# Adaptive modulation as a row product with an accumulating VectorE step, in a fused two-block transformer kernel

## The reference

```python
c_act = jax.nn.silu(c)                       # (1, 1024)
mod = jnp.einsum('bd,de->be', c_act, w_ada[l]) + b_ada[l]      # w_ada (1024, 6144)
shift_m, scale_m, gate_m, shift_f, scale_f, gate_f = jnp.split(mod, N_MOD, axis=-1)
h = (_rms(x) * (1.0 + scale_m) + shift_m)
...
x = x + gate_m * jnp.einsum('bse,ed->bsd', mixed, w_out[l])
h = (_rms(x) * (1.0 + scale_f) + shift_f)
u = jnp.square(jax.nn.relu(jnp.einsum('bsd,df->bsf', h, w_mlp_in[l])))
x = x + gate_f * jnp.einsum('bsf,fd->bsd', u, w_mlp_out[l])
```

## Time and profile before

| | |
|---|---|
| median of 3 runs | 836.43 us (834.17 to 836.99) |
| profiled execution, its own time | 834.69 us |
| its span, first to last instruction | 832.9 us |
| PE busy | 798.2 us, 6530 matmul records |
| PEld busy | 782.2 us |
| DVE busy | 625.4 us, 977 instructions |
| ACT busy | 377.0 us |
| DMA | 155.6 MB, mean 187 GB/s |
| mean granted clock of PE | 0.982 of full |

### The profile page before, as it was taken

How to read it: one execution, slowest core, us unless ns; L and a number is a source line. 1 busy time by engine, 2 the same in 40 slices (tenths; PEclk the granted TensorE clock), 3 DMA queues, 4 the chain that set the end, 5 groups by cost and what they waited for, 6 DMA issues and landing times.

```text
span 832.9 us, 15451 instructions
## 1 busy us (share of the span) xinstructions
PE 798.2 (96%) x6530; PEld 782.2 (94%) x6530; DVE 625.4 (75%) x977; ACT 377.0 (45%) x504; POOL 27.7 (3%) x27
## 2 busy tenths in 40 slices
PE   8997998998899999999999999999989899999998
PEld 8997997898898999999999999989889899999998
DVE  5957586876975778999997888967767778855563
ACT  6656334553755633343335553445446533434331
POOL 0000000002101000000000000300010000000000
PEclk9999997999999999999999999999899999999999
DMA  9854442221734447787886425554215257745521
GB/s 338 297 192 149 146 161 102 102 103 52 295 110 153 153 155 304 282 308 270 294 305 240 174 102 191 210 206 153 102 52 203 102 207 300 282 173 202 174 80 52
DMA packets 23972, 155.60 MB, mean 187 GB/s; under 512 B 3552, under 2 KB 3680, under 8 KB 5856
## 3 DMA queue, kind: packets, MB, share of 16 engines
q1 hardware_dynamic: 23904, 154.61, 51.3%
HBM read 153.55 MB, written 1.05 MB: 186 GB/s over the span
## 4 chain that ended last, share of the span: by engine, by line
PE 73%; DVE 11%; issue 8%; ACT 6%; DMA 1%; POOL 1%; SPq 0%; DVEq 0%; POOLq 0%; ACTq 0%
PE bank L740 13%; PE bank L742 13%; PE bank L741 13%; PE bank L809 7%; PE bank L812 7%; PE bank L811 7%; DVE sb_lo L1664 3%; ACT sb_hi L1339 3%; PE bank L748 2%; PE bank L1202 2%; PE bank L750 1%; PE bank L751 1%; DMA sb_raw<-in_stream 1%; PE bank L1226 1%; PE bank L1169 1%
## 5 line engine op out<-in xcount | busy, mean ns | idle before, releaser
L1664 DVE TENSOR_TENSOR sb_lo<-sb_raw,sb_hi 128x2048 fp32r<-128x2048 f32 (+1 forms) x116 | 261.6, 2258 | 96.8 <-ACT sb_hi L1339 96.4
L1339 ACT CAST sb_hi<-sb_raw 128x2048 fp32r<-128x2048 f32 (+1 forms) x116 | 217.5, 1880 | 112.1 <-PE bank L812 55.6
L740 PE MATMUL bank<-sb_u_hi,sb_hi 128*128 128x256 f32 (+2 forms) x800 | 230.9, 289 | 2.8 <-issue 2.8
L742 PE MATMUL bank<-sb_u_hi,sb_lo 128*128 128x256 f32 (+2 forms) x800 | 228.1, 285 | 0.0
L741 PE MATMUL bank<-sb_u_lo,sb_hi 128*128 128x256 f32 (+2 forms) x800 | 227.3, 284 | 0.0
L740 PEld LDWEIGHTS bank<-sb_u_hi,sb_hi 128*128 128x128 f32 (+2 forms) x800 | 152.4, 191 | 6.3 <-issue 5.5
L742 PEld LDWEIGHTS bank<-sb_u_hi,sb_lo 128*128 128x128 f32 (+2 forms) x800 | 152.9, 191 | 0.2
L741 PEld LDWEIGHTS bank<-sb_u_lo,sb_hi 128*128 128x128 f32 (+2 forms) x800 | 152.9, 191 | 0.3
L809 PE MATMUL bank<-sb_hid_hi,sb_hi 128*128 128x256 f32 x432 | 121.3, 281 | 0.4 <-DVE sb_hid_lo L1718 0.4
L812 PE MATMUL bank<-sb_hid_hi,sb_lo 128*128 128x256 f32 x432 | 120.8, 280 | 0.0
L811 PE MATMUL bank<-sb_hid_lo,sb_hi 128*128 128x256 f32 x432 | 120.5, 279 | 0.0
(11 more groups left out here) (352 smaller groups left out, 1229.5 us busy)
## 6 DMA issues: line engine op xcount, KB each, us to landing
sb_raw<-in_stream SPq DMA_DIRECT2D x140, 1024.0 KB, 5.0
sb_raw<-in_stream SPq DMA_DIRECT2D x4, 256.0 KB, 6.5
sb_raw<-in_stream SPq DMA_DIRECT2D x2, 512.0 KB, 9.2
sb_mem_t<-in_mem SPq DMA_DIRECT2D x1, 1024.0 KB, 4.9
out<-sb_h SPq DMA_DIRECT2D x4, 256.0 KB, 2.1
sb_const<-in_constants SPq DMA_DIRECT2D x1, 830.0 KB, 10.4
sb_h<-in_x SPq DMA_DIRECT2D x1, 576.0 KB, 3.8
sb_h<-in_x SPq DMA_DIRECT2D x1, 512.0 KB, 6.9
```

The costliest lines, as they stand in the source:

```text
L740: nc.tensor.matmul(out, a_hi, b_hi, start=(i == 0), stop=False)
L742: last = nc.tensor.matmul(out, a_lo, b_hi, start=False, stop=(i == n - 1))
L1339: nc.scalar.copy(hi[:, s % SPLIT, 0:n], x[:, 0:n]).then_inc(sem("hi_ready"), 1)
L1664: tt(lo[:, s % SPLIT, 0:n], x[:, 0:n], f32(hi[:, s % SPLIT, 0:n]), ALU.subtract) \
```

## The change

w_ada is laid out the other way round on the host: a block still holds 256 outputs, but the output is on the partition and the 1024 input features lie along it, two groups of 128 outputs beside each other. The row c is loaded into all 128 partitions (`c_row`, 128 by 1024, one DMA) and ACT applies silu to it. `ada(j)` on DVE is now two instructions, each 128 by 1024: the block times `c_row`, written back over the block, with the sum along the row written to one column of `mod`. The matmuls with ones and the DVE step behind them go; the biases are added by three instructions (`ada_bias`). The two pieces of the first projection go into the feed-forward, one more in round 2 and one more in round 9, so that rounds 2 to 9 have two each. `tail_t` and `logit_t` become views of a part of `summed`, to make room.

```diff
-    ada, summed = iter(range(24)), []
+    ada = iter(range(24))
     def more_ada():
-        if len(summed) == 2:
-            add("ada_sum", summed.pop(0))
         for j in ada:
             raw.append(("ada", j))
             add("ada", j)
-            summed.append(j)
             return
...
-    add("c_act")
     block("proj", 0, evac_now=False, ahead=False)
...
-    more_ada()
     block("proj", 3)
     add("rstd_row", 0)
     add("turn_qk", 0)
-    more_ada()
     block("proj", 4)
...
         if i == 1:
             add("hidden", hidden.pop(0))
+            add("c_act")
+            add("weigh_cols")
         if 2 <= i <= 9:
             more_ada()
         block("ffn_in", 2 * i + 1)
-        if 3 <= i <= 8:
+        if 2 <= i <= 9:
             more_ada()
         block("ffn_out", i - 1, hidden_first=i == 10)
         if i == 8:
+            add("ada_bias", 0, 12)
             add("mod", 0)
...
     block("proj2", 14, between=[("pv", 16), ("pv", 17)])
-    while summed:
-        add("ada_sum", summed.pop(0))
     steps([("turn_p", 18), ("turn_p", 19), ("scores", 20), ("scores", 21), ("mix_scale", 0, 1), ("mix_tanh", 0),
-           ("mod", 1), ("shift", 1)])
+           ("ada_bias", 12, 20), ("mod", 1), ("shift", 1)])
...
-        if 7 <= i < 9 and summed:
-            add("ada_sum", summed.pop(0))
+        if i == 8:
+            add("ada_bias", 20, 24)
...
+    def ada(j):
+        return w["w_ada_2"][0][:, 256 * j:256 * j + 256].reshape(D, 2, P).transpose(2, 1, 0).reshape(P, -1)
...
-        c_act = sb(ctx, "c_act", [P, KD])
-        c_tanh = sb(ctx, "c_tanh", [P, KD])
-        ada_acc = sb(ctx, "ada_acc", [P, 2, W_COLS])
+        c_row = sb(ctx, "c_row", [P, D])
...
+        tail_t = summed[0:TAIL, 1, :]
+        logit_t = summed[0:FH, 1, :]
...
-            def ada_sum(j):
-
-                pe.wait_ge(sem("ada_ready"), j + 1)
-                ps = claim(("ada_sum", j), "turn")
-                for m in range(2):
-                    last = nc.tensor.matmul(ps[:, m:m + 1], ada_acc[:, j % 2, m * P:m * P + P], ones[:, 0:1],
-                                            start=True, stop=True)
-                fill(last, ("ada_sum", j))
...
-                nc.scalar.activation(c_tanh[:, :], cols[:, c:c + KD], ACT.Tanh, scale=0.5) \
-                    .then_inc(sem("c_tanh_ready"), 1)
+                act.wait_ge(sem("c_loaded"), 16)
+                nc.scalar.activation(c_row[:, :], c_row[:, :], ACT.Silu).then_inc(sem("c_ready"), 1)
...
                 x = shaped(raw_ready(dve, ("ada", j)), ("ada", j))
-                acc = ada_acc[:, j % 2, :]
-                if j >= 2:
-                    wait_filled(dve, ("ada_sum", j - 2))
-                link(ts(acc, x[:, 0, :], c_act[:, 0:1], None, ALU.mult))
-                for k in range(1, KD):
-                    ins = stt(acc, x[:, k, :], c_act[:, k:k + 1], acc, ALU.mult, ALU.add)
-                    if k < KD - 1:
-                        link(ins)
+                if j == 0:
+                    dve.wait_ge(sem("c_ready"), 1)
+                for m in range(2):
+                    ins = stt(x[:, m, :], x[:, m, :], 1.0, c_row[:, :], ALU.mult, ALU.mult,
+                              accum_out=mod[:, 2 * j + m:2 * j + m + 1])
                 ins.then_inc(sem("ada_ready"), 1)
-            def ada_sum(j):
-                key = ("ada_sum", j)
-                ps = wait_filled(dve, key)
-                c = COL_AT["b_ada"] + 2 * j
-                free(tt(mod[:, 2 * j:2 * j + 2], ps[:, 0:2], cols[:, c:c + 2], ALU.add), key)
+            def ada_bias(j0, j1):
+
+                dve.wait_ge(sem("ada_ready"), j1)
+                c = COL_AT["b_ada"]
+                some = slice(2 * j0, 2 * j1)
+                link(tt(mod[:, some], mod[:, some], cols[:, c + 2 * j0:c + 2 * j1], ALU.add))
...
+                if i == 5:
+                    load(c_row[:, :], d["c_2"].rearrange("a c -> (a c)").partition_broadcast(P), "c_loaded")
```

More of the change, by code:

```diff
@@ L62 @@
 DECAY_AT = CONST_AT["decay"]
-COL_AT = dict(norm_mix=0, norm_mem_kv=8, norm_mem_q=16, norm_ffn=24, c=32, b_ada=40, pos_k=88, pos_v=104,
-              norm_final=120)
-NCOLS = 128
+COL_AT = dict(norm_mix=0, norm_mem_kv=8, norm_mem_q=16, norm_ffn=24, b_ada=32, pos_k=80, pos_v=96,
+              norm_final=112)
+NCOLS = 120
 def constants():
@@ L442 @@
               for c in (RQ, RK, FQ, FK, RV, RG, FV, FOG)}
-SMALL = ["cmp_w2_k", "cmp_w2_v", "b_forget_2", "q_norm_gain_2", "k_norm_gain_2", "fox_out_gain_2", "ret_out_gain_2"]
+SMALL = ["c_2", "cmp_w2_k", "cmp_w2_v", "b_forget_2", "q_norm_gain_2", "k_norm_gain_2", "fox_out_gain_2", "ret_out_gain_2"]
 def feature_major(a):
@@ L453, in columns_of @@
     source = dict(norm_mix=w["norm_mix"], norm_mem_kv=w["norm_mem_kv"], norm_mem_q=w["norm_mem_q"],
-                  norm_ffn=w["norm_ffn"], c=w["c_2"], b_ada=w["b_ada_2"], pos_k=w["cmp_pos_k"],
+                  norm_ffn=w["norm_ffn"], b_ada=w["b_ada_2"], pos_k=w["cmp_pos_k"],
                   pos_v=w["cmp_pos_v"], norm_final=w["norm_final"])
@@ L561, in two_blocks_kernel @@
         gates, qk_t, km_t, vm, sel_neg, cmp_in, kc_t, vc, w2k, w2v, hid_x, hid_t, hid_k, hid_v, cmp_s, cmp_m, \
-            cmp_d, gate_c, idx_w, best, tail_t = scope(
+            cmp_d, gate_c, idx_w, best = scope(
                 first, ("gates", [P, 24, T]), ("qk_t", [P, 14, T]), ("km_t", [P, 2, T]), ("vm", [P, 2, T]),
@@ L582, in two_blocks_kernel @@
         s.close()
-        ret_t, fox_t, proj2, gains, logit, soft, logit_t, fstat, decays = scope(
+        ret_t, fox_t, proj2, gains, logit, soft, fstat, decays = scope(
             second, ("ret_t", [P, 2 * RH, T]), ("fox_t", [P, 2 * FH, T]), ("proj2", [P, NT, PROJ2]),
-            ("gains", [P, 2 * HD + FH + 1024]), ("logit", [P, NT, FH]), ("soft", [P, NT, FH]), ("logit_t", [FH, T]),
+            ("gains", [P, 2 * HD + FH + 1024]), ("logit", [P, NT, FH]), ("soft", [P, NT, FH]),
             ("fstat", [P, 5, NT * FH]), ("decays", [P, RH * 2 * P]))
@@ L628, in shaped @@
                 return flat.rearrange("p (k n) -> p k n", k=16)
+            if kind == "ada":
+                return flat.rearrange("p (m k) -> p m k", m=2)
             n = width(s) if s is not None else 256
@@ L1305, in _ @@
                      cmp_scores=cmp_scores, turn_cmp_p=turn_cmp_p, cmp_pv=cmp_pv, scores=scores, turn_p=turn_p,
-                     pv=pv, turn_o=turn_o, ada_sum=ada_sum, forget=forget, forget_sum=forget_sum,
+                     pv=pv, turn_o=turn_o, forget=forget, forget_sum=forget_sum,
                      turn_fox=turn_fox, turn_ret=turn_ret, ret_scores=ret_scores, ret_pv=ret_pv,
@@ L2153, in ada @@
                 x = shaped(raw_ready(dve, ("ada", j)), ("ada", j))
-                acc = ada_acc[:, j % 2, :]
-                if j >= 2:
-                    wait_filled(dve, ("ada_sum", j - 2))
-                link(ts(acc, x[:, 0, :], c_act[:, 0:1], None, ALU.mult))
-                for k in range(1, KD):
-                    ins = stt(acc, x[:, k, :], c_act[:, k:k + 1], acc, ALU.mult, ALU.add)
-                    if k < KD - 1:
-                        link(ins)
-                ins.then_inc(sem("ada_ready"), 1)
-            def ada_sum(j):
-                key = ("ada_sum", j)
-                ps = wait_filled(dve, key)
-                c = COL_AT["b_ada"] + 2 * j
-                free(tt(mod[:, 2 * j:2 * j + 2], ps[:, 0:2], cols[:, c:c + 2], ALU.add), key)
+                if j == 0:
[3 more added lines that the diff above has]
+                              accum_out=mod[:, 2 * j + m:2 * j + m + 1])
+                ins.then_inc(sem("ada_ready"), 1)
+            def ada_bias(j0, j1):
[3 more added lines that the diff above has]
+                link(tt(mod[:, some], mod[:, some], cols[:, c + 2 * j0:c + 2 * j1], ALU.add))
             def modulation(i):
-                wait_evacuated(dve, ("ada_sum", 7 if i == 0 else 19))
                 new = mod[:, 24 * i + 8:24 * i + 16]
@@ L2299, in _ @@
                  "o_group": o_group, "merge": merge, "residual": residual,
-                 "final_norm": final_norm, "ada": ada, "ada_sum": ada_sum, "mod": modulation,
+                 "final_norm": final_norm, "ada": ada, "ada_bias": ada_bias, "mod": modulation,
                  "fox_square": fox_square, "fox_norm": fox_norm, "forget": forget, "log_f": log_f, "forget_sum": forget_sum,
```

14 lines of the change are left out of this document (4 added, 10 removed).

## The result

The changed kernel takes **814.06 us** (812.07 to 815.46), where the kernel before takes 835.48 in the same comparison: a ratio of 0.975, with a 95% interval of 0.973 to 0.978, or 21.4 us. Direction and mechanism were as forecast, but 821.0 was 7 us too high and 817.0, the lower end of the range, was passed by 3. The profiled executions are a closer measure of the parts: their spans are 832.9 and 812.4 us, 20.5 apart, where the sum on record had 15.4.

What follows compares the result with a forecast made beforehand. PE was taken to bound the kernel; gains of 6.2 + 1.8 + 0.9 + 1.0 + 0.9 + 2.2 + 2.4 = 15.4 us took 834.69 to 819.3, put at a median of 821.0. The range was 817.0 to 828.0.

Steps and rivals of the forecast that it cites:

- the sum on record: Whole kernel: all forecast gains added up, 15.4 us.
- What bounds the kernel: Whole kernel: PE busy 798.2 of 832.9 us, so whatever leaves PE's chain shortens the kernel.
- 22 simple terms: Sums removed from PE: 14 feed-forward, 4 MLP, proj2 6 and 10, 0.44 us each; proj2 4 and 11, 1.0 and 0.9.
- DVE: Feed-forward rounds: a new piece takes 2.8 us, DVE's round 15.8 under PE's 17.1, so pieces cost nothing.
- The second rival: New DVE step with accumulator runs at half rate, a piece 5.0 us, median 845.6; chance 0.09.
- The clock behind the wait: Behind proj2 14: granted clock 0.50 for 6.57 us, blamed on the near-idle stretch; removing it gains 2.4 us.
- the 0.7 for DVE's backlog: Behind proj2 14: waiting on DVE's residue that may come back, up to 1.3 us, taken as 0.7.
- the wait of 2.24: Behind proj2 14: transposes start at 583.39 instead of 585.63, a gain of 2.2 us.
- the first rival: The clock falls all the same, the 2.4 us are lost, median 823.4; chance 0.20.
- The credit to the sums alone: Behind proj2 14: removing two sums was to end the wait, 2.2 us, and the clock's fall, 2.4 us.
- At no cost: First projection's pieces, rounds 2 and 9, row load, ACT step, bias additions, memset, buffer views: no change in time.
- Rivals 3 and 4: Feed-forward: loads come late, median 828.2, chance 0.04; no gain as DVE already sets it, median 827.2, chance 0.04.

Runs made afterwards that it cites:

- a_twice: Changed kernel with the two DVE steps of each of the feed-forward's 16 pieces executed twice; 838.41 us, 24.4 more.
- a_sums: Changed kernel with all 24 pairs of matmuls with ones put back at their old places, results unused; 824.59 us, 10.5 more.
- a_shift32: Changed kernel with 32 bytes of padding ahead of the buffers of the stages; 820.23 us, 6.2 more.
- b_shift928: Kernel before with 928 bytes of padding, putting hid at the changed kernel's place within 1024 bytes; 828.28 against 833.55 us.
- the probes: Two kernels of matmuls alone, streamed operand at 32 places; 0.1177 to 0.1200 us apart nearly everywhere, 0.1134 at place 576 in the second.
- a_u_fast: Changed kernel with u and hid at place 64 within 256 bytes, own u buffers for the MLP, shift columns written later; 819.98 us.
- a_u_fast2: Changed kernel with u and hid at place 64 within 256 bytes, own MLP u buffers, shift columns written ahead of out2 0; 808.70 us.
- a_u_place: Changed kernel with u groups 1024 bytes apart, u and hid at place 64 within 256, 48 shift-column products as separate matmuls; 819.68 us.

## Why the prediction was wrong, point by point

- *What bounds the kernel*: right. PE is the bound at nearly every place where a sum stood, and each of the 22 simple terms was within 0.1 us of its measured size.
- *DVE*: right in sign and cheaper than taken. 2.8 us for a piece were forecast, 2.4 measured; the lower bound, two plain operations, was the true value. It changed nothing in the sum, since either size lay under PE's products. The second rival did not come true. The rule of the Trainium skill on which it rested (page "Vector Engine (DVE) Microarchitecture Reference", section "Points that are easy to get wrong": half throughput for this shape with two sources in SBUF that are not bf16) is not what this case's trace shows: 1218 ns with two float32 sources and the accumulator on, 1224 without. Here the measurement decides. `a_twice` shows that the rival's price was about right, had the rate been halved: a round of 19.7 us with a piece of 4.8, where the text had 20.2 with one of 5.0.
- *The clock behind the wait*: the mechanism was right, the term mis-sized. 3.1 - 0.7 = 2.4 was taken, and 3.2 measured (5.46 less the wait of 2.24); the 0.7 for DVE's backlog was a guess between 0 and 1.3 and nothing came back. Together with the wait it was 5.46 for 4.6. That the clock falls all the same, the first rival, did not happen. The credit to the sums alone was incomplete, as `a_sums` shows.
- *"At no cost"*: this is the step that failed. The text looked at what each edit does to queues and engines, and said of the buffers only that the views are free when used. It did not ask what the new buffers do to the addresses of those behind them. So the time of the products that stream hid, which the sum put at no change, fell by 4.0 us (hid from 0.1169 to 0.1138). That an address alone does this is shown by `a_shift32`, which loses the 4.0 and 2.2 more by moving 32 bytes, and by `b_shift928`, which gains 5.3 in the kernel before. It is not the whole account: the rates also differ at one place, for a reason that stays open.
- *Range and conversion*: 15.4 + 4.0 + 0.9 = 20.3, the 20.5 of the spans. Against the profiled time of 834.69 that is 814.2; the measured median is 814.06. The forecast added 1.7 us for the distance between the profiled execution and the median of three; the changed kernel's profiled execution (814.58) lies 0.5 above its median, so this correction missed by 2. The lower end, 817.0, allowed for the clock and not for anything outside the listed terms. With the place in mind, a lower end of 812 would have been honest, and a higher upper end as well: the move of 32 bytes in `a_shift32` costs 6 us. (The chances that the text counts as faster add up to 0.925, where it says 0.91.)
- *Rivals 3 and 4*: neither showed. The feed-forward moved 294 GB/s at a DMA share of 0.81, and PE waited for no load; DVE has gaps now (142.4 of 166 us busy).

## What to carry to other kernels

Where one engine is full, an instruction costs its distance in that engine's row of start times, not its length, and 22 such terms added up here to within a tenth of a microsecond each. Setting the n-th matmul of one profile against the n-th of the other shows where a difference arises, including the part that no one had thought of. And a change that adds or drops a buffer moves all buffers behind it: before crediting an edit with a gain of half a per cent, pad it back to the old addresses and see what is left. Here only the reverse was done, the kernel before padded to the new place.

## What was not expected of the hardware

- The distance of matmuls that stream 256 float32r columns depends on where the streamed operand starts: in the probes 0.1177 to 0.1200 us at full granted clock with a period of 256 bytes, and no other engine at work. A faster rate, 0.1134, is seen at some of the places and only at times: the same block at the same address had 0.1177 in `a_u_fast` and 0.1134 in `a_u_fast2`. One rate holds for a whole block of products, and what picks it stays open.
- DVE's multiply of two float32 operands in SBUF with the sum accumulated costs 1218 ns for 128x1024, and the readout 83 ns; ACT's readout was 187 ns.
- A wait of PE with nearly no work in it was followed by a granted clock of 0.50 in both cases looked at above, for 6.6 us behind one of 2.2 us and for at least 16 us behind one of 5.6 us. But such a wait isn't needed: in `a_u_place` the clock fell to 0.50 for 20 us though PE had been busy for 5.00 of the 6 us shown in front of it.
